# Order of products in the projection tiles of a hybrid attention and HGRN2 encoder layer: 512-column products first, 256-column ones after them

## What is computed

```
xn = rmsnorm(x, norm_pre_w)                      # (256, 2048)
h = xn @ w_in                                    # (2048, 13312): q,k,v,z | hq,f_fwd,f_bwd,i,hz | gates
o_a = neighbourhood_attention(q, k, v) * silu(z)
o_b = rmsnorm(hgrn2_both_directions(hq, f_fwd, f_bwd, i)) * silu(hz)
g_a, g_b = sigmoid(gates + b_gate)
y = g_a * (o_a @ w_branch[:1024]) + g_b * (o_b @ w_branch[1024:])
out = x + rmsnorm(y @ w_out, norm_post_w)
```

## Time and profile before

| what | value |
|---|---|
| median of 3 runs | 833.8 us (830.61 to 833.92) |
| profiled execution, its own time | 832.17 us |
| its span | 830.2 us |
| granted TensorE clock, mean | 0.997 of full |
| TensorE busy | 820.4 us, 99% of the span |
| weight loads busy | 704.2 us, 85% |
| VectorE busy | 628.5 us, 76% |
| ScalarE busy | 409.0 us, 49% |
| DMA | 154.01 MB, mean 186 GB/s |

### The profile page before, as it was taken

One profiled execution on the slowest core, in us unless ns is written; L12 is line 12 of the kernel. 1 busy time (PEld: TensorE's weight loads), 2 busy tenths in 40 slices (PEclk: granted clock), 3 DMA queues, 4 the chain that ended last, 5 costly groups with the idle time before them and its releaser, 6 DMA issues.

```text
span 830.2 us, 13692 instructions
## 1 busy us (share of the span) xinstructions
PE 820.4 (99%) x5582; PEld 704.2 (85%) x5582; DVE 628.5 (76%) x1053; ACT 409.0 (49%) x690; POOL 41.6 (5%) x48
## 2 busy tenths in 40 slices
PE   9999999999999999999999999999999999999996
PEld 7888888888888888888888888888888888888884
DVE  4777658888888888888888888888785778765543
ACT  6745545445445445445445445445444545544442
POOL 5000100000001001000000000100000000000002
PEclk9999999999999999999999999999999999999998
DMA  9756867676576576576576576575575866676522
GB/s 333 277 170 191 215 186 181 171 194 168 163 195 169 163 196 167 163 196 167 163 200 168 159 201 166 161 201 154 153 197 158 241 175 193 201 261 225 183 93 101
DMA packets 246733, 154.01 MB, mean 186 GB/s; under 512 B 15288, under 2 KB 228368, under 8 KB 246288
## 3 DMA queue, kind: packets, MB, share of 16 engines
q1 hardware_dynamic: 245664, 149.17, 63.3%
q10 hardware_dynamic: 1008, 3.98, 1.3%
HBM read 151.04 MB, written 2.10 MB: 184 GB/s over the span
## 4 chain that ended last, share of the span: by engine, by line
PE 98%; DMA 1%; POOL 0%; ACT 0%; DVE 0%; POOLq 0%; issue 0%; ACTq 0%
PE psum L1150 47%; PE psum L1152 24%; PE psum L1203 3%; PE psum L1387 3%; PE psum L1204 3%; PE psum L1388 3%; PE psum L1389 3%; PE psum L1205 3%; PE psum L1256 1%; PE psum L1244 1%; PE psum L1219 1%; PE psum L1289 1%; PE psum L1232 1%; PE psum L1279 1%; DMA big<-in_x 1%; PE psum L1167 0%
## 5 line engine op out<-in xcount | busy, mean ns | idle before, releaser
L1150 PE MATMUL psum<-act_hl,w_hi 128*128 128x512 f32 x1408 | 500.5, 400 | 0.0
L1152 PE MATMUL psum<-act_hl,w_lo 128*128 128x256 f32 x1408 | 395.1, 281 | 0.0
L691 DVE TENSOR_TENSOR w_lo<-raw,w_hi 128x1024 fp32r<-128x1024 f32 x272 | 325.2, 1233 | 78.0 <-ACT w_hi L437 77.9
L1150 PEld LDWEIGHTS psum<-act_hl,w_hi 128*128 128x128 f32 x1408 | 264.8, 188 | 62.7
L437 ACT ACTIVATE w_hi<-raw 128x1024 fp32r<-128x1024 f32 x272 | 273.5, 1052 | 39.0 <-PE psum L1389 27.2
L1152 PEld LDWEIGHTS psum<-act_hl,w_lo 128*128 128x128 f32 x1408 | 266.4, 189 | 0.0
L451 ACT ACTIVATE part<-psum 128x256 f32<-128x256 f32 x88 | 33.6, 382 | 206.4 <-PE psum L1152 206.4
L1150 PE MATMUL psum<-branch_hl,w_hi 128*128 128x512 f32 x256 | 90.6, 399 | 0.0
L1152 PE MATMUL psum<-branch_hl,w_lo 128*128 128x256 f32 x256 | 72.0, 281 | 0.0
L1150 PEld LDWEIGHTS psum<-branch_hl,w_hi 128*128 128x128 f32 x256 | 48.2, 188 | 12.0
L1203 PE MATMUL psum<-w_hi,branch_hl 128*128 128x512 f32 x128 | 50.3, 393 | 0.2 <-DVE branch_hl L982 0.2
(11 more groups left out here) (135 smaller groups left out, 696.6 us busy)
## 6 DMA issues: line engine op xcount, KB each, us to landing
raw<-in_w_in SPq DMA_DIRECT2D x103, 1024.0 KB, 5.8
raw<-in_w_branch SPq DMA_DIRECT2D x16, 1024.0 KB, 5.9
raw<-in_w_out SPq DMA_DIRECT2D x16, 1024.0 KB, 5.1
bias_t<-in_na_rel_bias SPq DMA_DIRECT2D x32, 96.0 KB, 6.0
big<-in_x SPq DMA_DIRECT2D x4, 512.0 KB, 8.6
big<-in_x ACTq DMA_DIRECT2D x2, 1024.0 KB, 5.9
out<-big SPq DMA_DIRECT2D x5, 256.0 KB, 2.4
raw<-in_w_in SPq DMA_DIRECT2D x2, 512.0 KB, 6.8
```

Of the source, the lines that this page charges most:

```text
L691: nc.vector.tensor_tensor(w_lo[:, i, :], raw[:, r, 1024 * h:1024 * (h + 1)], w_hi[:, i, :].bitcast(F32), ALU.subtract).then_inc(lo_ready, 1)
L1150: nc.tensor.matmul(sums[h][:, :], w_hi[:, i, w], operand[:, k, :], start=first, stop=False, skip_group_check=True)
L1152: ins = nc.tensor.matmul(sums[h][:, 0:T], w_lo[:, i, w], operand[:, k, 0:T], start=False, stop=last, skip_group_check=True)
```

## The change

In `project` the pairs are taken apart. All sixteen 512-column products (both halves) are issued first, each half behind a wait for `hi_ready`. Then comes `between()`, and then the sixteen 256-column products, each half behind a wait for `lo_ready`. `half_used` is counted up after each half's 256-column products. In branch tiles `between()` keeps its place before the second half's first product, which is now the ninth 512-column product. The numbers of products and loads, and their operands, stay the same.

```
                 for h in range(2):
-                    if h == 1:
+                    pe.wait_ge(hi_ready, n * 2 + h + 1)
+                    if h == 1 and not whole:
                         between()
+                    i, blocks = half(h)
+                    for k, w in blocks:
+                        nc.tensor.matmul(sums[h][:, :], w_hi[:, i, w], operand[:, k, :], start=k == 0 if whole else k % 8 == 0,
+                                         stop=False, skip_group_check=True)
+                if whole:
+                    between()
+                for h in range(2):
                     pe.wait_ge(lo_ready, n * 2 + h + 1)
-                    i = (2 * r + h) % HALVES
-                    for kk in range(8):
-                        k = 8 * h + kk
-                        first, last = (k == 0, k == KT - 1) if sums[0] is sums[1] else (kk == 0, kk == 7)
-                        w = slice(kk * P, (kk + 1) * P)
-                        nc.tensor.matmul(sums[h][:, :], w_hi[:, i, w], operand[:, k, :], start=first, stop=False,
-                                         skip_group_check=True)
+                    i, blocks = half(h)
+                    for k, w in blocks:
                         ins = nc.tensor.matmul(sums[h][:, 0:T], w_lo[:, i, w], operand[:, k, 0:T], start=False,
-                                               stop=last, skip_group_check=True)
+                                               stop=k == KT - 1 if whole else k % 8 == 7, skip_group_check=True)
                     ins.then_inc(half_used, 1)
```

More of the change, by code:

```diff
@@ L1138, in project, with half @@
             def project(n, r, sums, operand, between):
+                def half(h):
+                    return (2 * r + h) % HALVES, [(8 * h + kk, slice(kk * P, (kk + 1) * P)) for kk in range(8)]
+                whole = sums[0] is sums[1]
                 for h in range(2):
-                    if h == 1:
+                    pe.wait_ge(hi_ready, n * 2 + h + 1)
+                    if h == 1 and not whole:
                         between()
-                    pe.wait_ge(lo_ready, n * 2 + h + 1)
-                    i = (2 * r + h) % HALVES
-                    for kk in range(8):
-                        k = 8 * h + kk
-                        first, last = (k == 0, k == KT - 1) if sums[0] is sums[1] else (kk == 0, kk == 7)
-                        w = slice(kk * P, (kk + 1) * P)
-                        nc.tensor.matmul(sums[h][:, :], w_hi[:, i, w], operand[:, k, :], start=first, stop=False,
-                                         skip_group_check=True)
+                    i, blocks = half(h)
[5 more added lines that the diff above has]
+                for h in range(2):
+                    pe.wait_ge(lo_ready, n * 2 + h + 1)
+                    i, blocks = half(h)
+                    for k, w in blocks:
                         ins = nc.tensor.matmul(sums[h][:, 0:T], w_lo[:, i, w], operand[:, k, 0:T], start=False,
-                                               stop=last, skip_group_check=True)
+                                               stop=k == KT - 1 if whole else k % 8 == 7, skip_group_check=True)
                     ins.then_inc(half_used, 1)
```

## The result

| | before | after |
|---|---|---|
| median of 6 runs each | 831.37 us (830.61 to 833.92) | 826.73 us (826.25 to 827.5) |
| profiled execution: time, span | 832.17, 830.2 us | 826.77, 824.8 us |
| projection stage (first L1150 to the first product of the last stage) | 634.58 us | 628.95 us |

The ratio is 0.9944, with a 95% interval of 0.9932 to 0.9955. The change makes the kernel faster by 0.56%, 4.6 us. The forecast was 825.9 us, on a median of three runs of the kernel before that was 2.4 us above that of six, and against the profiled execution's own time 7.9 us less where 5.4 were measured (832.17 - 826.77). All of it lies in the projection stage: 634.58 - 628.95 = 5.63 us. One execution in what follows, of `e_between_late`, took 894.42 us in a slower state of the chip and is left out of its median.

What follows compares the result with a forecast made beforehand. TensorE's own stream, busy 99% of the span, was taken as the bound. 832.2 - 8.7 (5.2 ns on 1,664 pairs) + 0.8 (wait) gave 824.3 us, or 825.9 on the median of runs; range 816 to 837.

Steps and rivals of the forecast that it cites:

- The likeliest case: Projection stage: runs of equal products shorten TensorE's stream, 256-column products at 118 to 123 ns; 825.9 us, chance 0.38.
- order costs and gives nothing: Rival: each projection product has its price wherever it stands, only the wait is added; 834.6 us, chance 0.22.
- the load shows: Rival: 256-column runs go at the weight load's pace; at 130 ns each, 842.6 us; chance 0.09.
- The 256-column product: Projection tiles: 120 ns each in a run, 13.3 ns fixed cost on top of 106.7 ns streaming.
- shorter yet: Rival: the 256-column product costs 116.5 ns in its run, or less down to 111; 820.1 us, chance 0.27.
- The 512-column product: Projection tiles: 226.7 ns each in a run of its like, priced from quiet stretches of the last stage.
- The wait for `ob_lo`: First branch tile: TensorE reaches this wait earlier and waits once for VectorE, 0.7 to 0.8 us; plus 0.8 us.
- The rule quoted from the Trainium skill: TensorE's warm products take N/2.4 + 2.5 ns; a pair would cost 325 ns in either order, the change nothing.
- Breaks, halves, small products later, branch tiles' late release: Loads after breaks, earlier tile starts, small products 0.8 us later, branch first-half copies 1.8 us later: each costed at zero.
- The slow rhythm will go with the alternation: Projection pairs ran at 353.7 or 346.7 ns; the slower, some 7 ns more, was expected to vanish in runs.
- theory A: Follow-up expectation: first five 512-column products behind a 256-column run cost 232 ns, the rest 226.5, 256-column ones 119.5.
- Theory H: Follow-up expectation: breaks leave 512-column products at 232 ns, a run of some eight heals this, pairs keep what they meet.

Runs made afterwards that it cites:

- `e_between_late`: Kernel before the change, pairs kept, with the groups' small products moved three pairs back, behind the eleventh pair; 831.44 us, ratio 1.0.
- `e_groups8`: Kernel before, with eight 512-column then eight 256-column products in each half, small products and waits where they were; 827.65 us, ratio 0.9935.
- `e_lo384`: Changed kernel with the low-weight product over 384 columns instead of 256, more work than needed; span 918.6 us.
- `e_narrow_lo`: Changed kernel with only 64 of the 128 weight columns in each 256-column product, part of the result left out; span 816.5 us.
- `e_pairs_narrow_hi`: Kernel before, in pairs, with only 64 of 128 weight columns in each 512-column projection product, part of the result left out; span 811.0 us.
- `e_narrow_hi`: Changed kernel with only 64 of 128 weight columns in each 512-column projection product, part of the result left out; span 827.4 us.
- `e_first_branch`: Changed kernel, but in the first branch tile both products of the first half come before the wait for `ob_lo`; 825.94 us, ratio 0.9932.
- `e_healed_pairs`: Kernel before, reordered per tile: eight 512-column products, eight pairs mixing the two halves, then eight 256-column products; 831.33 us, ratio 0.998.

## Why the prediction was right, and where its sum was off

*The likeliest case came.* The time is 826.7 us against 825.9. That they lie 0.8 us apart is luck in part: the forecast was a fall of 7.9 us, measured are 4.6 in the medians and 5.6 in the stage, and the median of three runs from which it started was 2.4 us high. The sign and the cause (runs of equal products) are as forecast, and the rivals "order costs and gives nothing" and "the load shows" didn't come. A 256-column product in its run is at 119.5 ns, far below the 127.2 at which the balance would have turned. That the place of the small products gives nothing is shown by `e_between_late`, and that neither it nor the waits for `hi_ready` are needed by `e_groups8`.

*The 256-column product:* 119.5 ns measured, 120.0 forecast. The number was right, and its ground in part. I took 13.3 ns on top of the columns as a fixed cost, the same for both widths. With a full load behind each product the steady intervals bear this out at three widths: 120.0, 173.3 and 226.7 ns for 256, 384 and 512 columns (`e_lo384` has the middle one), each 13.3 above the columns divided by 2.4 GHz. But it isn't fixed whatever the load: `e_narrow_lo` and `e_pairs_narrow_hi` show 113.3 to 113.8 once the load behind 256 columns is half as long. Half a load behind 512 columns took nothing off (229.8 ns in `e_narrow_hi`), and that stays unexplained. The rival "shorter yet" isn't met in long runs. Its 116.5 ns (116.6 by the trace of before) is undercut in runs of two, at 115.4.

*The 512-column product* is the term that was mis-sized: "in a run of its like: 226.7 ns". It is 228.4 over a tile, since the first five behind another kind of product cost 232, more than the 230 that I had named as a sign of being wrong. (228.4 - 226.7) x 1,664 = 2.8 us of the 8.7 didn't come. The price was from the middle of a stage of such products only the earlier trace rows; the start of that stage, in the same trace, had intervals of 232. In this kernel a run is sixteen long, so its start counts.

*The sum, with what was measured:* 351.9 - (228.4 + 119.5) = 4.0 ns x 1,664 = 6.7 us, less 0.95 for the wait, is 5.7. The stage gave 5.6.

*The wait for `ob_lo`:* 0.7 us of idle time, forecast at 0.7 to 0.8. The forecast left out the slow restart behind it. `e_first_branch` shows that it was a loss of its own: without it the stage is 0.95 us shorter, which is what the starts in the timeline say too.

*The rule quoted from the Trainium skill* ("TensorE: Matmul & The Clock Gate", "Back-to-back issue gap") is met neither in size nor in the price's being the same "whatever follows", which was my reading. The section gives the formula for an isolated product and says that in a stream of loads and products both set the spacing. This is such a stream. The pair fell from 351.9 to 347.9 ns by the order alone, not to 325.

*Breaks, halves, small products later, branch tiles' late release:* costed at zero, and TensorE waits for no one in the groups or the later branch tiles. What the prediction puts at stake at the breaks is 42 x 0.09 = 3.8 us, not 3.

*"The slow rhythm will go with the alternation"* was right for sixteen in a row, but the reason that I gave (short and long cover in turn) is only partly borne out. Halving either load removes the rhythm in pairs, so it needs both loads at full length, also the one with 100 ns to spare. Its dependence on the group size has no simple course:

| products of one width in a row | stage, us | ratio to before (interval) |
|---|---|---|
| 1 (before) | 634.58 | 1 |
| 2 | 629.16 | 0.9937 (0.9922 to 0.9951) |
| 4 | 632.11 | 0.9967 (0.9954 to 0.998) |
| 8 | 630.20 | 0.9935 (0.9919 to 0.9952) |
| 16 (changed; the stage holds the 0.95 us of the wait) | 628.95 | 0.9944 (0.9932 to 0.9955) |

The two products taken apart, as the mean interval from the start of each, without breaks, show where the turn comes from:

| in a row | 512 columns, ns | 256 columns, ns | together |
|---|---|---|---|
| 1 (before) | 235.3 | 116.6 | 351.9 |
| 2 | 233.2 | 115.4 | 348.6 |
| 4 | 232.0 | 118.3 | 350.3 |
| 8 | 230.1 | 119.0 | 349.1 |
| 16 (changed) | 228.4 | 119.5 | 347.9 |

The 512-column product gets cheaper with every step. The 256-column one gets dearer from two on: in twos the first takes 114.7 ns and the second 116.1, in fours they take 117 to 119, and in sixteens all but the first two take 120.0. Going from two to four, it loses 2.9 ns where the 512-column product gains 1.2. So theory A's price of 512 columns (232 in the first five) holds at 2 as well, and what it misses there is the 256-column product. Why the first products of a run are cheap or dear, why the slow rhythm sets in, and why some breaks lead to the fast one, stays open. Theory H describes the breaks and fails in `e_healed_pairs`.

## What to carry to other kernels

Where TensorE is the bound and its products have two widths, each with a load of its own, price them from start to start in runs of their kind, and look at the first products of a run apart from the rest. Grouping equal products is worth nearly 1% of such a stage here and needs no large groups: two in a row gave as much as sixteen, within the intervals. Not every size does as well: four in a row gave 0.4%. Before moving a wait ahead in TensorE's stream, count what stood between it and its releaser; one tile with both products of its first half ahead of the wait took the loss away.

## What the runs showed that I had not expected

- At the full granted clock and with a load of 128 weight columns behind each, fp32r products of 256, 384 and 512 columns settle at 120.0, 173.3 and 226.7 ns. That is the columns divided by 2.4 GHz (106.7, 160.0 and 213.3) and the same 13.3 ns for each (`after`, `e_lo384`). With 64 weight columns behind 256 columns it is 113.3, half of the excess (`e_narrow_lo`).
- A load of 128 weight columns behind a 256-column product costs 6 to 7 ns more than one of 64, though loads follow each other at 111 ns elsewhere.
- Halving the load of the 512-column products made the changed kernel slower (229.8 ns for each, span 827.4 against 824.8), and the kernel before faster (span 811.0 against 830.2). The same edit has opposite signs in the two orders. The slower 512-column product in the changed kernel is not explained.
- A run of 512-column products behind a narrower kind starts with a loss of 26 to 40 ns, whether 256 columns with half loads (26) or full ones (28) or 384 columns (40) stood ahead of it.
